# Attention probabilities divided on VectorE and transposed in transposing mode, in place of a product with a diagonal of reciprocals

## What is computed

```python
q = _rms(q.reshape(B_, S, N_HEADS, HEAD_DIM), gain_q)
k = _rms(k.reshape(B_, S, N_HEADS, HEAD_DIM), gain_k)
s = einsum('bhqd,bhkd->bhqk', q, k) * HEAD_DIM ** -0.5 - slopes * dist
s = where(allowed, s, NEG_INF)          # causal; in layer 1 also the indexer's 64 best keys
p = softmax(s, axis=-1)
o = einsum('bhqk,bhkd->bhqd', p, v)
y = concatenate([other_mixer, o], axis=-1)
x = x + gate_res * ((y * silu(g)) @ w_out[l])
```

## Time and profile before

| | |
|---|---|
| three executions | 1022.77, 1023.13, 1023.72 us |
| median | 1023.13 us |
| span of the profiled execution | 1022.7 us |
| PE busy in it | 961.2 us |
| DVE busy | 835.0 us |
| ACT busy | 437.6 us |

### The profile page before, as it was taken

One profiled execution on the slowest core, in us unless ns is written; L12 is line 12 of the kernel. 1 busy time (PEld: TensorE's weight loads), 2 busy tenths in 40 slices (PEclk: granted clock), 3 DMA queues, 4 the chain that ended last, 5 costly groups with the idle time before them and its releaser, 6 DMA issues.

```text
span 1022.7 us, 20334 instructions
## 1 busy us (share of the span) xinstructions
PE 961.2 (94%) x7776; PEld 952.6 (93%) x7776; DVE 835.0 (82%) x1244; ACT 437.6 (43%) x693; POOL 46.7 (5%) x63
## 2 busy tenths in 40 slices
PE   5197799999999999999999999999999999999997
PEld 5197699999999999999999999999999999999997
DVE  4898987987889778887877898888999886878842
ACT  3132125434555444433344444444445554743331
POOL 1000000001010000000000000000010100000000
PEclk9997798999999999999999999999999999999999
DMA  9999888889776788899857755644445455588961
GB/s 334 324 331 344 320 301 317 321 287 370 285 280 230 278 273 288 315 350 361 318 194 267 239 195 178 192 137 160 159 154 183 157 174 194 191 308 305 335 227 45
DMA packets 71095, 261.34 MB, mean 256 GB/s; under 512 B 7904, under 2 KB 8032, under 8 KB 70768
## 3 DMA queue, kind: packets, MB, share of 16 engines
q1 hardware_dynamic: 68544, 250.86, 69.4%
q0 software_dynamic: 2480, 9.50, 2.6%
HBM read 256.07 MB, written 4.19 MB: 254 GB/s over the span
## 4 chain that ended last, share of the span: by engine, by line
PE 79%; DVE 10%; DMA 6%; issue 2%; ACT 1%; SPq 0%; DVEq 0%; POOL 0%; ACTq 0%; POOLq 0%
PE bank L708 20%; PE bank L709 19%; PE bank L710 19%; DMA ada<-ada_units 6%; DVE acc L1040 5%; PE bank L810 3%; PE bank L813 3%; PE bank L812 3%; DVE wlo L1029 3%; PE bank L845 1%; PE bank L725 1%; PE bank L778 1%; PE bank L727 1%; PE bank L728 1%; PE bank L762 1%
## 5 line engine op out<-in xcount | busy, mean ns | idle before, releaser
L401 ACT ACTIVATE whi<-raw 128x1024 fp32r<-128x1024 f32 x282 | 297.2, 1060 | 453.1 <-PE bank L710 335.0
L1029 DVE TENSOR_TENSOR wlo<-raw,whi 128x1024 fp32r<-128x1024 f32 x282 | 341.6, 1223 | 93.5 <-ACT whi L401 93.0
L708 PE MATMUL bank<-hhi,whi 128*128 128x256 f32 x1168 | 337.1, 289 | 2.7 <-DVE wlo L1029 1.0
L709 PE MATMUL bank<-hlo,whi 128*128 128x256 f32 x1168 | 330.4, 283 | 0.0
L710 PE MATMUL bank<-hhi,wlo 128*128 128x256 f32 x1168 | 330.3, 283 | 0.0
L1040 DVE SCALAR_TENSOR_TENSOR acc<-ada,cact,acc 128x1024 f32<-128x1024 f32 x176 | 226.1, 1285 | 36.4 <-DMA ada<-ada_units 20.5
L708 PEld LDWEIGHTS bank<-hhi,whi 128*128 128x128 f32 x1168 | 223.9, 192 | 6.1 <-issue 3.8
L709 PEld LDWEIGHTS bank<-hlo,whi 128*128 128x128 f32 x1168 | 224.1, 192 | 0.1
L710 PEld LDWEIGHTS bank<-hhi,wlo 128*128 128x128 f32 x1168 | 223.9, 192 | 0.0
L708 PE MATMUL bank<-ghi,whi 128*128 128x256 f32 x512 | 147.9, 289 | 0.0
L709 PE MATMUL bank<-glo,whi 128*128 128x256 f32 x512 | 144.9, 283 | 0.0
(11 more groups left out here) (166 smaller groups left out, 1082.1 us busy)
## 6 DMA issues: line engine op xcount, KB each, us to landing
raw<-w_slabs SPq DMA_DIRECT2D x282, 512.0 KB, 4.7
ada<-ada_units SPq DMA_DIRECT2D x192, 512.0 KB, 6.3
X<-xT SPq DMA_DIRECT2D x1, 2048.0 KB, 7.5
x_dram<-X POOLq DMA_DIRECT2D x4, 512.0 KB, 5.4
outT<-X POOLq DMA_DIRECT2D x4, 512.0 KB, 5.6
V<-pool_w POOLq DMA_DIRECT2D x1, 1024.0 KB, 5.4
U<-xT POOLq DMA_DIRECT2D x2, 512.0 KB, 9.0
V<-xT POOLq DMA_DIRECT2D x2, 512.0 KB, 4.8
```

Of the source, the lines that this page charges most:

```text
L401: act.activation(whi[:, slot], raw[:, slot], ACT.Copy).then_inc(hi_done, 1)
L708: mm(out, whi[:, s, k, :], ahi[:, c, :], start=(c == 0), stop=False)
L709: mm(out, whi[:, s, k, :], alo[:, c, :], start=False, stop=False)
L1029: dve.tensor_tensor(wlo[:, s], raw[:, s], whi[:, s].bitcast(F32), ALU.subtract)\
```

## The change

PD and its semaphore `pdiag` go. `divide` multiplies the exponentials in SP by the reciprocals in place, in a 128x128 and a 128x256 scaling that each count `p_scaled` up by one, and PE transposes the three blocks of SP with `nc.tensor.transpose` and `ident`. What PE writes to PT, and all that follows, stays.

```diff
--- before.py
+++ after.py
@@ -119,7 +119,6 @@
         SG = sb("SG", [P, 2, SEQ])
         SP = sb("SP", [P, 2, KEYS])
         PTs = sb("PTs", [P, 2, KEYS])
-        PD = sb("PD", [P, 2, QT, P])
         KD = sb("KD", [P, QT, P])
         D = sb("D", [P, KEYS])
         MK = sb("MK", [P, KEYS])
@@ -193,7 +192,7 @@
         d_ready, pool_mm, pool_out = sem("d_ready"), sem("pool_mm"), sem("pool_out")
         kdiag, kb_done, kmul = sem("kdiag"), sem("kb_done"), sem("kmul")
         ds_ready, scored, s_added, max_done = sem("ds_ready"), sem("scored"), sem("s_added"), sem("max_done")
-        exp_done, pdiag, pt_done, pt_copied = sem("exp_done"), sem("pdiag"), sem("pt_done"), sem("pt_copied")
+        exp_done, p_scaled, pt_done, pt_copied = sem("exp_done"), sem("p_scaled"), sem("pt_done"), sem("pt_copied")
         pv_done, o_copied = sem("pv_done"), sem("o_copied")
         u_done = sem("u_done")
         wt_done, wi_ready = sem("wt_done"), sem("wi_ready")
@@ -836,14 +835,13 @@
                         .then_inc(scored, 1)
                 if 0 <= i - 1 < HC:
                     a = HC * layer + i - 1
-                    pe.wait_ge(pdiag, a + 1)
+                    pe.wait_ge(p_scaled, 2 * (a + 1))
                     if a:
                         pe.wait_ge(pt_copied, a)
                     else:
                         pe.wait_ge(pool_out, HC)
-                    for out, keys, q in ((0, 0, 0), (P, P, 1), (2 * P, 2 * P, 1)):
-                        ins = mm(PT[:, out:out + P], SP[:, a % 2, keys:keys + P], PD[:, a % 2, q, :],
-                                 start=True, stop=True)
+                    for keys in range(0, KEYS, P):
+                        ins = nc.tensor.transpose(PT[:, keys:keys + P], SP[:, a % 2, keys:keys + P], ident[:])
                     ins.then_inc(pt_done, 1)
                 if 0 <= i - 2 < HC:
                     a, h = HC * layer + i - 2, i - 2
@@ -1220,9 +1218,10 @@
                     dve.wait_ge(exp_done, 2 * (a + 1))
                     seq(dve.reciprocal(rl[:, i % 2, :], ls[:, i % 2, :]))
                     settle()
-                    for q in range(QT):
-                        ins = dve.tensor_scalar(PD[:, i % 2, q, :], ident[:], rl[:, i % 2, q:q + 1], None, ALU.mult)
-                    ins.then_inc(pdiag, 1)
+                    for q, (c0, c1) in enumerate(((0, P), (P, KEYS))):
+                        ins = dve.tensor_scalar(SP[:, i % 2, c0:c1], SP[:, i % 2, c0:c1], rl[:, i % 2, q:q + 1],
+                                                None, ALU.mult)
+                        ins.then_inc(p_scaled, 1)
 
             plan = conv_plan()
             taps = [0]
```

## The result

The changed kernel takes 1017.75 us (median of four executions, 1015.35 to 1018.61) beside 1023.38 us for the kernel before in the same comparison (1022.77 to 1023.72). The ratio is 0.9945, 95% interval 0.9928 to 0.9961: 5.6 us faster, with 4.0 to 7.4 us inside the interval. The forecast was 3.0 us and the range began at 1018.0.

A forecast was written before the change was run, and what follows sets the result against it. The prediction took PE (busy 94%) as the bound, with DVE (82%) close behind; gains of 1.2 us in layer 0 and 1.8 in layer 1 took 3.0 off 1023.1, giving 1020.1 us, range 1018.0 to 1022.5.

The forecast's parts named there:

- Three passes for six: PE, each of 16 head steps: three one-pass transposes replace six multiplication passes, saving 0.33 us a head, 5.3 us at most.
- Rival (e): PE's transposes take half of 0.11 us, so eight heads without a wait give 0.17 more each: 1018.8 us; chance 0.02.
- Layer 0 1.2 us: First layer's eight head steps: ideal gain 2.67 us, less 1.5 lost where PE waits for DVE, leaves 1.2.
- Layer 1 1.8 us: Second layer's eight head steps: ideal gain 2.67 us, less 0.85 lost in heads 5 to 7, leaves 1.8.
- Head 3's transfer: Layer 0: DVE's second ada unit can't come sooner than its transfer, so PE, 0.8 us earlier, loses 0.3 us.
- The scaling, 0.12 us more: DVE, each head: the 128x256 scaling on SP takes 407 ns, making the pair 0.12 us longer, 2.0 us in all.
- The restart, 0.1 us: PE, where it has to wait for DVE's second scaling: the group then takes 0.94 instead of 0.83 us, 0.1 more.
- The clock: Attention stretches: forecast stays at 1.00; a rival had PE fall to 1.2 GHz, 3.5 us each fall, 1027 us, chance 0.05.
- The sum: Both layers' attention: gains of 1.2 and 1.8 us make 3.0 us, 1020.1 us; chance 0.60.
- rival (a): Both layers' attention: DVE never limits and transfers move along, so all 5.3 us come through, 1017.8 us; chance 0.12.

## Why the prediction was wrong

- **Three passes for six, 0.33 us a head: right.** 48 records, 0.11 us apart; heads 0 to 4 give 0.34 each, but for head 1 of layer 0. The four times that the Trainium skill gives in "TensorE: Matmul & The Clock Gate", Terms, are not found: two times again, 0.33 for 0.67 us. Rival (e), which rested on them, had 4.3 us for its number, what the stretches gained, and that is luck: its condition, transposes closer than 0.11 us, did not occur.
- **Layer 0 1.2 us: mis-sized, measured 2.03. Layer 1 1.8 us: mis-sized, 2.25.** The mechanism is the one forecast, PE running into DVE in head 1 and heads 5 to 7, and the losses were put too high at each: by step, predicted loss and the one measured against 0.34 a head, head 1 0.2 and 0.10; head 3 0.3 and 0.0; head 5 0.34 and 0.24; head 6 0.5 and 0.35; head 7 0.13 and 0.01; layer 1 head 5 0.2 and 0.10, heads 6 and 7 0.63 and 0.35. Together 2.3 us were forecast and 1.15 measured.
- **Head 3's transfer: the step that failed.** I read DVE's 0.46 us before the second ada unit as a late transfer that keeps its time. That unit's DMA was issued more than 10 us earlier: in the trace after, SP's queue issues the two units at 289.38, and they are used at 299.9 and 301.64. Both have landed by 296.2 (second fence below), 5 us before the use. The 0.46 us is the same in ten traces whose starts lie 4.7 us apart, and moves with DVE's stream. The profile names DVE itself as the releaser, which I had overridden. In these ten traces it stands before the same instruction of DVE, with 306 others before it. In the kernel with doubled scalings six more lie before that unit, and the idle time there is 0.10 us, as between other pairs of units. So it belongs to a place in DVE's program and not to the transfer; what happens there stays open, and no experiment was made for it.
- **The scaling, 0.12 us more: mis-sized.** 347 ns, so 0.07. I had this as the lower bound and took the row of a form with two scalar operands (407 ns, L1235) over one of another width with none. The new form has one, and takes 60 ns more for 256 columns than for 128. The estimate of 350 ns that I had set aside was the right one; its slope is 200 / 384 = 0.52 ns a column and not the 0.55 that I wrote, and no run shows its split into 154 and 200 ns.
- **The restart, 0.1 us: mis-sized.** It is 0.10 only in the old form; with one pass a transpose it is 0.06. Heads that waited before have the smaller restart in place of the larger, so that head 7 of layer 0 gains 0.33 in spite of a longer scaling.
- **The clock: right.** 1.00 through both stretches, with three transposes a step and waits of up to 0.8 us.
- **The sum.** 3.0 was forecast, 4.3 is what the change does to the attention stretches in three traces. The prediction priced head 3's transfer at 0.3 and the cheaper scaling at 0.6; with both it would have said 3.9, and the time of 1023.1 - 4.3 = 1018.8 lies in its range. The median of the first comparison, 5.6, holds about 1.3 us more, and but for the first of the kernel before, which lay within 1 us, the executions of one and the same program lie 3 to 10 us apart; in the profiles most of what differs arises before 160 us. I had said that a measurement tells 2 us from no change, from three executions that lay within 1 us; I did not put this into the range. That the range missed, by 0.25 us, comes from both together.
- **The rival (a), 5.3 us,** has the nearer number to 5.6 but not the reason: 1.15 us of the 5.44 is lost at DVE, with waits in seven heads (eight had been forecast, with head 3). Its mechanism becomes true when `divide` is moved.

SP's queue in the trace after, to the third point, and the time to landing of these two transfers:

```profile
289.38 0.92 SPq L255 DMA_DIRECT2D ada<-ada_units  x2
```
```profile
DMA to landing us min/median/max: 4.5/5.4/6.2
```

## What to carry to other kernels

Where the critical engine gains per step and another engine sits close behind, go through the steps one by one, but before calling an idle time fixed by a transfer, check the named releaser and when the transfer landed. A result that is due at the start of the next step, and whose inputs are ready in this one, belongs in this one: the move was worth 2.0 us on the old kernel and 3.2 on the new, and left the engine's load unchanged. When the effect is the size of the variation between executions, compare the starts of the same instruction in two traces: that gave 4.29, 4.29 and 4.27 us, where medians gave 5.6, 5.1 and 3.7 us.

## What the runs showed of the hardware

From one start to the next a 128x128 fp32 transpose takes PE 0.11 us, in one record with a weight load of 140 ns, where the fp32 multiplication takes 0.22 us in two records with 191 ns. A tensor_scalar with one column scalar on 256 fp32 columns took 347 ns and on 128 columns 287; with two column scalars 256 columns took 407. In two profiles of the kernel before, PE's first attention matmul lay 4.7 us apart, of which 4.6 had arisen before 160 us; the attention stretches repeated to 0.01 us, and the passage between the layers was 0.2 us shorter. Over all eleven traces that passage, which no edit touches, lay from 1.3 us below to 0.6 above the first trace's. DVE had one idle time of 0.46 us, for which no wait for another engine or a transfer shows, before the same instruction of its stream in ten traces; with six more instructions before it, it was gone.
